# Mixing matmuls of the spatial gating, moved between the tiles of the projection that follows

## The reference, cut to what matters

```python
proj = h @ w_in[l]
q, k, v, g, u, vs, p, gate_cols = split_columns(proj)
...
def spatial_gating(u, v, w_s, b_s, v_gain):
    u = jax.nn.gelu(u)
    v = rms_norm(jax.nn.gelu(v), v_gain)
    vc = v.reshape(B, nc, CHUNK, GMLP_GROUPS, GMLP_GROUP_DIM)      # chunks of 128 tokens, 4 groups
    w = jnp.where(mask[None], w_s, jnp.zeros_like(w_s))            # 128 x 128 for each group, causal
    mixed = jnp.einsum('gts,bnsgc->bntgc', w, vc) + b_s.T[None, None, :, :, None]
    return u * mixed.reshape(B, S, GMLP_WIDTH)
...
y_pool = multiscale_pool(p, w_pool[l], b_pool[l], pool_scale[l])
```

## Time and profile before

| | us |
|---|---|
| median of three runs | 3637.46 (3636.68 to 3638.87) |
| the profiled execution | 3638.44, of which its span 3636.8 |
| TensorE matmuls busy | 3357.8 (92%) |
| VectorE busy | 1968.3 (54%) |
| ScalarE busy | 1129.3 (31%) |
| HBM traffic | 354 MB read, 98 GB/s over the span |

### The profile page before, as it was taken

One profiled execution on the slowest core, in us unless ns is written; L12 is line 12 of the kernel. 1 busy time (PEld: TensorE's weight loads), 2 busy tenths in 40 slices (PEclk: granted clock), 3 DMA queues, 4 the chain that ended last, 5 costly groups with the idle time before them and its releaser, 6 DMA issues.

```text
span 3636.8 us, 45188 instructions
## 1 busy us (share of the span) xinstructions
PE 3357.8 (92%) x14884; PEld 2727.3 (75%) x14884; DVE 1968.3 (54%) x2794; ACT 1129.3 (31%) x1514; POOL 160.2 (4%) x200
## 2 busy tenths in 40 slices
PE   5899999999998899899999997998999889989998
PEld 4568777878886577787878886766788777867886
DVE  5365447664444455547564445455755643467655
ACT  2123323322332123333322232252333322333333
POOL 1000000000001000000000001021000102110000
PEclk7999999999999999899999998998999999989999
DMA  6116423522222125323422221201222322113222
GB/s 224 52 58 197 161 74 116 175 87 95 96 98 82 41 89 194 133 87 128 167 81 98 94 97 62 75 18 58 98 93 96 107 71 86 47 35 103 94 92 75
DMA packets 98228, 357.68 MB, mean 98 GB/s; under 512 B 11104, under 2 KB 11120, under 8 KB 97856
## 3 DMA queue, kind: packets, MB, share of 16 engines
q1 hardware_dynamic: 97344, 353.73, 29.0%
q0 software_dynamic: 768, 2.47, 0.2%
HBM read 354.06 MB, written 2.10 MB: 98 GB/s over the span
## 4 chain that ended last, share of the span: by engine, by line
PE 75%; DVE 9%; issue 6%; DVEq 3%; POOLq 3%; ACT 2%; DMA 1%; ACTq 0%; POOL 0%; SPq 0%
PE pb L426 21%; PE pb L427 20%; PE pb L428 20%; POOLq L352 2%; PE pb L481 2%; PE pb L483 2%; PE pb L482 2%; DMA raw<-stream 1%; DVEq L1571 1%; DVE yL L1269 1%; PE pb L814 1%; PE pb L541 1%; DVE act L1572 1%; DVE act L1574 1%; DVE tab L1675 1%
## 5 line engine op out<-in xcount | busy, mean ns | idle before, releaser
L426 PE MATMUL pb<-hH,hi 128*128 128x512 f32 x2400 | 951.0, 396 | 48.8 <-DVEq L1303 27.4
L1222 DVE TENSOR_TENSOR lo<-raw,hi 128x1024 fp32r<-128x1024 f32 x549 | 688.3, 1259 | 536.8 <-ACT hi L876 466.4
L427 PE MATMUL pb<-hL,hi 128*128 128x512 f32 x2400 | 944.5, 394 | 0.0
L428 PE MATMUL pb<-hH,lo 128*128 128x512 f32 x2400 | 943.4, 393 | 0.0
L876 ACT ACTIVATE hi<-raw 128x1024 fp32r<-128x1024 f32 x549 | 577.2, 1053 | 265.7 <-PE pb L483 97.8
L426 PEld LDWEIGHTS pb<-hH,hi 128*128 128x128 f32 x2400 | 458.0, 191 | 153.0 <-issue 25.5
L426 PE MATMUL pb<-yH,hi 128*128 128x512 f32 x1344 | 526.0, 391 | 20.5 <-DVEq L1270 18.0
L427 PEld LDWEIGHTS pb<-hL,hi 128*128 128x128 f32 x2400 | 457.8, 191 | 96.0 <-issue 1.0
L428 PEld LDWEIGHTS pb<-hH,lo 128*128 128x128 f32 x2400 | 457.0, 190 | 96.4
L427 PE MATMUL pb<-yL,hi 128*128 128x512 f32 x1344 | 524.8, 390 | 0.0
L428 PE MATMUL pb<-yH,lo 128*128 128x512 f32 x1344 | 524.5, 390 | 0.0
(11 more groups left out here) (269 smaller groups left out, 2965.1 us busy)
## 6 DMA issues: line engine op xcount, KB each, us to landing
raw<-stream SPq DMA_DIRECT2D x664, 512.0 KB, 3.3
x<-xT SPq DMA_DIRECT2D x1, 2048.0 KB, 8.9
outT<-act SPq DMA_DIRECT2D x8, 256.0 KB, 2.2
tab<-decay SPq DMA_DIRECT2D x1, 1024.0 KB, 5.6
scr<-ws POOLq DMA_DIRECT2D x2, 256.0 KB, 4.3
scr<-bs POOLq DMA_DIRECT2D x2, 256.0 KB, 6.2
tab<-tables POOLq DMA_DIRECT2D x1, 512.0 KB, 3.7
cst<-consts SPq DMA_DIRECT2D x1, 302.0 KB, 3.2
```

What stands on the lines that cost most here:

```text
L426: pe.matmul(out, whi, ahi, start=first, stop=False)
L427: pe.matmul(out, whi, alo, start=False, stop=False)
L428: return pe.matmul(out, wlo, ahi, start=False, stop=last)
L1222: dve.tensor_tensor(lo[:, s], raw[:, s], hi[:, s].bitcast(F32), ALU.subtract).then_inc(lo_ready, 1)
```

## The change

TensorE now issues two mixing steps, then a tile of `p`, then the third mixing step, a tile, the fourth, and so on; the last two tiles follow the eighth step. VectorE takes its tick for the projection after each mixing step instead of after all eight. ScalarE waits, before it stores tile n of `p`, for the split of step n alone. The loops over the `p` tiles are written out on all three engines. SyncE and GpSimd have the same program as before. The products computed are the same.

```diff
@@ TensorE @@
                 pe.wait_ge(ws_ready, l + 1)
                 pe.wait_ge(v_normed, vn.next(4))
-                for n in range(KT):
+
+                def mix_tile(n):
 
                     pe.wait_ge(mix_free, mix.next())
                     for t in range(TT):
...
                     ins.then_inc(mix_full, 1)
-                tiles_T(8, hH, hL, None)
+
+                mix_tile(0)
+                mix_tile(1)
+                for n in range(KT):
+                    tile_T(n % RING, hH, hL)
+                    if n + 2 < KT:
+                        mix_tile(n + 2)
                 gated_pairs()
@@ ScalarE @@
-                def drain_p(i, s):
-                    act.wait_ge(y_ready, l * 56 + 16)
-                    drain_to(0, ACT.Copy)(i, s)
-                tiles_T(8, drain_p, uses_st=False)
+                for n in range(KT):
+                    s = n % RING
+                    tick(s)
+                    act.wait_ge(tile_done, done.next())
+                    act.wait_ge(y_ready, l * 56 + (8 + n + 1))
+                    act.activation(A[:, n], pb[:, s], ACT.Copy).then_inc(bank_free, 1)
                 pairs()
@@ VectorE @@
                     dve.tensor_tensor(A[:, n], A[:, n], pv, ALU.mult)
                     dve.drain().then_inc(mix_free, 1)
                     halves(A[:, n], yH[:, n], yL[:, n])
-                tiles_T(8, None)
+                    tick(n % RING)
+                    drained.next()
```

## The result

The changed kernel takes 3615.36 us (median of five runs, 3611.05 to 3619.02), the kernel before 3638.87 us (five runs, 3636.68 to 3646.18). The ratio is 0.9929, with a 95% interval of 0.9915 to 0.9942: faster by 0.7%, 21 to 31 us. A second series, on another occasion, gave 0.9913 (0.9896 to 0.9929), 3612.27 against 3644.09 us. The forecast was 3610 us, in a range of 3605 to 3618. A single execution out of all, of a kernel with the order of before, took 5712 us at a mean granted clock of 0.562 and is in none of the comparisons.

The account below looks back on a forecast made before the run. TensorE, busy 92% of the span, was taken as the bound, idling in the mixing behind VectorE. Tiles 43.4 plus steps 7.3 us make 50.7 us a layer, saving 27.9 us in all: 3610 us, range 3605 to 3618.

Parts of the forecast that it names:

- The hole and its cause: Mixing, 449.6 to 472 us: TensorE's later steps wait for VectorE, which starts one every 3.07 us.
- The sum: Mixing and `p` tiles: 43.4 us of tiles plus 7.3 us of steps, 50.7 us a layer; gain 27.9 us together.
- The spacing of the stores: ScalarE's stores of `p`: 6.3 us apart for tiles 1 to 5, 5.4 us for the last two.
- The clock: TensorE in the whole mixed stage: granted clock 1.00, the 2.4 GHz level, once the gaps are gone.
- The slack behind VectorE: Mixed stage: VectorE's step n+2 ends near D + 5.9, needed not before D + 12.7; slack 6.8 us.
- The fall of the clock: Rival, eight `p` tiles: clock drops to 1.2 GHz; with all eight 34 us a layer slower, about 3706 us; chance 3%.
- Costly steps: Rival, mixing steps: low clock or costly borders, up to 2.08 us each, 3610 to 3629 us; chance 6%.
- A new wait in the chain of ticks: Rival, hand-overs among ScalarE, VectorE, TensorE: 0.5 us lost on each of 16 tiles, 3618 us; chance 6%.
- That the gain does not arrive: Rival: the stage was not on the path, something else starts the pairs; time stays 3637 us; chance 2%.
- the comparison of executions: Whole time: setting the gain against the execution of before adds a spread of 1 to 2 us.
- One of the signs of being wrong: First stage's end to span's end: a distance other than 3122.2 us less the second layer's gain.
- Code: Written-out loops, some 100 more TensorE instructions and one branch fewer: 0, between -1 and +1.6 us for both layers.

Follow-up runs that it names:

- the run with three tiles in front: Changed kernel with steps interleaved between the first tiles only and VectorE's ticks behind all its steps; median 3640.95 us, ratio to the kernel before 0.9988.
- the first filled run: Kernel before with mixing steps 1 to 7 issuing their matmuls three times; stage 64.62 us, ratio to the kernel before 0.9999.
- one step of lead: Changed kernel with mixing step n+1 instead of n+2 behind tile n; median 3613.1 us, ratio to the kernel before 0.9924.
- the run with the code alone: Kernel before, its order kept, with the loops over the `p` tiles written out on three engines; ratio to the kernel before 1.0015.

## Why the prediction was right

**The hole and its cause** were read rightly. VectorE's period of 3.07 us made it; with the tick moved it closes, and with the tick left behind (the run with three tiles in front) the same wait appears one place further on.

**The sum.** Predicted 50.7 us for the stage, measured 50.74 in each layer, in both profiles of the changed kernel. Its terms hold one by one: a tile 5.44 us where no step follows (5.43), a step 6.34 - 5.44 = 0.90 to 0.91 us. The price taken from `spread_c` was the right row: neither the bound of 0.98 us for entry and exit nor the low-clock 2.08 us came in. The spacing of the stores was miscounted: six of them (tiles 1 to 6) and not five come 6.3 us after the one before, and only the last comes 5.4 us after it. The sum counts steps and does not rest on it. Doubling the steps priced them a second time, at 0.89 us.

**The clock**: 1.00 in the stage, as from the earlier trace rows. Its share in the hole of before, put at the first tile alone (1.4 us in the expectation of the first filled run), is 1.9 us with the last step's low-clock excess; the prediction said of that step that its length cost nothing, since VectorE's period covered it. That holds for the steps ahead of it, not for the last, which has the first tile behind it. The sum did not rest on it.

**VectorE, ScalarE, the transfers**: nothing that TensorE waited for in the stage, as worked out. The slack behind VectorE was real: one more split was free, three more cost TensorE 3.9 us a layer. The count that what comes out of a step is needed two tiles later was more than was needed; one step of lead does as well.

**The rivals** all stayed away. The fall of the clock: 1.00, and still with twice the float32 matmuls. The Trainium skill, page "TensorE: Matmul & The Clock Gate", section "A second HAM failure mode: psum-queue depth-cycling", puts the oscillation down to small idle times between groups that cycle through banks. Here the groups cycle through six banks with no idle time between them, so the cause that it names did not occur and its rule was not put to the test. Costly steps: 0.90 us. A new wait in the chain of ticks: none, and still none with a use one tile after the step (one step of lead); TensorE does wait with three more splits. That the gain does not arrive: it does.

**What was off: the comparison of executions.** The forecast of 3610 us is 5.4 us below the median of 3615.36, and that median lies outside the 3606 to 3614 us to which the forecast gave its 83%. That it lies inside 3605 to 3618 is luck: the range was drawn that wide for a wait in the chain of ticks, and there was none. The step that failed is the one that set the sum against the profiled execution of before and gave "the comparison of executions 1 to 2" us. That rested on three runs within 2.2 us of each other. With more runs the kernel before lies between 3630 and 3650 us, and its medians in four series between 3639 and 3644. The profiled execution was 6.6 us shorter than usual behind the second stage and some 3.3 us longer than the changed kernel's between the stages. One of the signs of being wrong came with it: the first stage's end to the end of the span is 3613.7 - 502.06 = 3111.6 us, and not 3122.2 - 13.9 = 3108.3. The differences outside the stages make these 3.3 us (6.6 more behind the second, 3.3 less between). The gain itself, 27.8 us by the stages, lies inside both intervals: 21 to 31 us from the first series, 26 to 38 us from the second.

**Code**, put at 0 between -1 and +1.6 us, cost nothing in the stage. On the whole time the run with the code alone was 2 to 9 us slower than before by its interval, so the term is not shown to hold there.

## What to carry to other kernels

Where an engine's work for the next stage is queued behind its work for this one, the others stand still once the tiles made ahead are used up. Interleave on both sides: the consumer's preparation of the next tiles must move together with the producer's order, or the wait only moves. Price the inserted work from a row where the same instruction already stands in a full stream, and check the engine between against the new period, 4.2 us against 6.34 here. Measure a stage on the engine that bounds it: the stores of another engine can lag, as by 9 us with three more splits, and then show a loss that is not there.

## What the runs showed of the hardware

- A float32 matmul of 128x128 in a full stream costs 0.22 to 0.23 us, as much as one 128x512 pass of the split form (0.227 us), and changing from one form to the other and back seven times in a layer costs nothing that can be seen (0.90 us for a step with its borders, 0.89 us for the same four without).
- Float32 matmuls in a row keep TensorE at its 2.4 GHz level (granted clock 1.00, also in the filled steps, three of which had an idle time of 0.13 us ahead of them); with idle times of 0.94 us and more ahead of short steps it fell to the 1.2 GHz level.
- The same program, 0.2 us apart in two executions at 3112 us, lost 6.6 us more in one of them behind that, most of it between 3115 and 3265 us, where its granted clock was lower (0.94 and 0.83 against 1.00 and 0.94 in the first 60 us). A profile of one execution can be 7 us from the next in parts that nobody touched, so parts have to be compared, not spans.
